# Split-precision mixing and feed-forward products: high and low parts of the activations side by side, five matmuls per step in place of six

## The reference

```python
u = rmsnorm(x, norm_attn); proj = u @ w_in          # attention heads, indexer, state-space heads
h = x + jnp.concatenate([att, y], axis=-1) @ w_out  # mixing product, 2048 x 2048
f = rmsnorm(h, norm_ffn)
h = h + (jax.nn.silu(f @ w_gate) * (f @ w_up)) @ w_down   # hidden width 5632
y = rmsnorm(h, norm_final)
```

## Time and profile before

| | us |
|---|---|
| median of 3 runs | 3274.39 |
| lowest, highest | 3269.07, 3275.76 |
| the profiled execution | 3267.44 |
| its span, first to last instruction | 3265.6 |
| mean granted clock of TensorE | 0.956 |

### The profile page before, as it was taken

How to read it: one execution, slowest core, us unless ns; L and a number is a source line. 1 busy time by engine, 2 the same in 40 slices (tenths; PEclk the granted TensorE clock), 3 DMA queues, 4 the chain that set the end, 5 groups by cost and what they waited for, 6 DMA issues and landing times.

```text
span 3265.6 us, 53293 instructions
## 1 busy us (share of the span) xinstructions
PE 3057.1 (94%) x21743; PEld 2899.3 (89%) x21743; DVE 957.0 (29%) x1714; ACT 763.0 (23%) x1171; POOL 981.5 (30%) x406
## 2 busy tenths in 40 slices
PE   6999997899999996899999999999999999999997
PEld 6887996687777784899999999999999999999997
DVE  2322797434333432212221221221212121121223
ACT  4223222222222222223212121212121112112122
POOL 2322332111111110233333333333333333333331
PEclk8999998998889996899999999999999999999998
DMA  6322223444444443432222222222222222222221
GB/s 186 109 66 72 92 92 91 115 131 139 129 126 117 115 126 114 139 100 93 78 78 86 96 78 78 78 84 98 78 78 78 86 96 78 78 78 89 93 91 59
DMA packets 350273, 317.78 MB, mean 97 GB/s; under 512 B 39821, under 2 KB 319413, under 8 KB 348808
## 3 DMA queue, kind: packets, MB, share of 16 engines
q1 hardware_dynamic: 319368, 293.93, 29.0%
q10 hardware_dynamic: 30720, 21.05, 2.1%
HBM read 284.90 MB, written 31.43 MB: 97 GB/s over the span
## 4 chain that ended last, share of the span: by engine, by line
PE 57%; issue 34%; POOL 7%; ACTq 1%; DVE 1%; ACT 0%; POOLq 0%; DVEq 0%
PE G L705 40%; PE G L1117 17%; POOL WL L634 4%; POOL WL L663 3%; ACTq L1167 0%; ACTq L1168 0%; DVE us L2016 0%; DVE y_out L2035 0%; POOL WL L655 0%; ACT WRAW L1176 0%; PE B L720 0%; ACTq L39 0%; DVE gs L1987 0%; ACT XR L1181 0%; DVE hl L2022 0%
## 5 line engine op out<-in xcount | busy, mean ns | idle before, releaser
L705 PE MATMUL G<-AH,WH 128*128 128x288 f32 (+1 forms) x5024 | 1090.4, 299 | 42.0 <-DVE us L2016 12.2
L705 PE MATMUL G<-AL,WH 128*128 128x288 f32 (+1 forms) x5024 | 1077.9, 296 | 0.0
L705 PE MATMUL G<-AH,WL 128*128 128x288 f32 (+1 forms) x5024 | 1076.5, 296 | 0.0
L705 PEld LDWEIGHTS G<-AH,WH 128*128 128x128 f32 (+1 forms) x5024 | 814.2, 191 | 69.4 <-issue 51.3
L705 PEld LDWEIGHTS G<-AL,WH 128*128 128x128 f32 (+1 forms) x5024 | 814.9, 190 | 0.0
L705 PEld LDWEIGHTS G<-AH,WL 128*128 128x128 f32 (+1 forms) x5024 | 813.4, 190 | 0.0
L655 POOL TENSOR_TENSOR WL<-WRAW,WH 128x1024 fp32r<-128x1024 f32 x208 | 517.4, 2488 | 943.6 <-ACT WH L648 943.6
L648 ACT CAST WH<-WRAW 128x1024 fp32r<-128x1024 f32 x208 | 218.5, 1051 | 1006.6 <-PE G L705 900.1
L653 POOL TENSOR_TENSOR WL<-WRAW,WH 128x1024 fp32r<-128x1024 f32 x88 | 210.8, 2395 | 357.9 <-ACT WH L646 357.9
L1117 PE MATMUL G<-hh,WH 128*128 128x288 f32 x1408 | 303.0, 296 | 4.6 <-DVE hl L2022 4.6
L1117 PE MATMUL G<-hl,WH 128*128 128x288 f32 x1408 | 300.3, 294 | 0.0
(11 more groups left out here) (308 smaller groups left out, 2018.9 us busy)
## 6 DMA issues: line engine op xcount, KB each, us to landing
WRAW<-in_w_gate SPq DMA_DIRECT2D x22, 2048.0 KB
WRAW<-in_w_up SPq DMA_DIRECT2D x22, 2048.0 KB
WRAW<-in_w_down SPq DMA_DIRECT2D x22, 2048.0 KB
WRAW<-in_w_in SPq DMA_DIRECT2D x14, 2048.0 KB, 8.6
raw<-in_w_in SPq DMA_DIRECT2D x48, 512.0 KB, 4.0
kca<-in_cache_k SPq DMA_DIRECT2D x256, 64.0 KB, 2.0
vca<-in_cache_v SPq DMA_DIRECT2D x256, 64.0 KB, 2.0
WRAW<-in_w_out SPq DMA_DIRECT2D x16, 1024.0 KB
```

Source lines behind the costliest of these rows:

```text
L705: last = nc.tensor.matmul(G[gslot][0:width, h, 0:HALF], wt[:, half, k % 8, 0:width], act[:, (k + shift) % KT, h * HALF:(h + 1) * HALF], st ...
```

## The change

AH and AL become one array A3 of 16 blocks x 3 x 384 (WIDE = 384, REST = 96), on the same bytes; hh and hl become H3. A block's three rows hold: 288 high and 96 low values, 288 high and 96 low, 384 low (`highs`, `lows`). Per step, the high weights meet the three rows of 384 (three matmuls into three PSUM banks), the low weights the 288 high values of the first two (two matmuls): `wide_steps`. A result tile F[0] or F[1] has three banks, F[0] being two of the old four single banks with one of G; highs(F) holds the products with high activations, lows(F) those with low ones, and VectorE adds the two. Between dependent VectorE instructions there are new waits (`link`, `Steps` on lo_added). The first mixing tile waits for one more taken tile, the second for the last attention copies; the transposes back use two banks for m < 3. The diff, without its unchanged surroundings and the list of semaphores:

```diff
@@ -18,6 +18,8 @@
 HALF = NT // 2
+WIDE = 2 * NT // 3
+REST = WIDE - HALF
 NH, DH = 8, 128
...
@@ -176,6 +178,9 @@
         top[0] = max(spot["hl"][1], spot["mx"][1])
+        A3 = sb("A3", [P, KT, 3, WIDE], F32R, at=spot["AH"][0])
+        H3 = sb("H3", [P, 4, 3, WIDE], F32R, at=spot["hh"][0])
+        assert spot["A3"][1] == spot["AL"][1] and spot["H3"][1] == spot["hl"][1]
         xt = sb("xt", [P, 2, NT])
...
@@ -187,8 +192,10 @@
-        G = [ctx.enter_context(nc.psum_tensor(f"G{i}", [P, 2, 512], F32)) for i in range(2)]
-        B = [ctx.enter_context(nc.psum_tensor(f"B{i}", [P, 512], F32)) for i in range(4)]
+        PS = ctx.enter_context(nc.psum_tensor("PS", [P, 8, 512], F32))
+        G = [PS[:, 2 * i:2 * i + 2, :] for i in range(2)]
+        B = [PS[:, 4 + i, :] for i in range(4)]
+        F = [PS[:, 3:6, :], PS[:, 0:3, :]]
...
@@ -296,7 +303,7 @@
             for t in range(5):
-                plan(("y", m, t), (5 * m + t) % 4)
+                plan(("y", m, t), 2 + t % 2 if m < 3 else t % 4)
...
@@ -706,6 +713,36 @@
+        def highs(v):
+
+            return v[:, 0:2, 0:HALF]
+
+        def lows(v):
+
+            return v[:, 0:2, HALF:WIDE], v[:, 2, 0:WIDE].rearrange("p (a b) -> p a b", a=2)
+
+        def by_half(v):
+
+            v = v.rearrange("p (a b) -> p a b", a=2)
+            return v[:, :, 0:REST], v[:, :, REST:HALF]
+
+        def wide_steps(out, wh, wl, act, first, last_k):
+
+            for c in range(3):
+                ins = nc.tensor.matmul(out[:, c, 0:WIDE], wh, act[:, c, :], start=first, stop=last_k and c == 2)
+            for c in range(2):
+                ins = nc.tensor.matmul(out[:, c, 0:HALF], wl, act[:, c, 0:HALF], start=False, stop=last_k)
+            return ins
+
+        def wide_half(pe, c, half, slot, shift=0, ready=None):
+
+            pe.wait_ge(s["w_lo"], c + 1)
+            for k in range(8 * half, 8 * half + 8):
+                if ready:
+                    ready(k)
+                last = wide_steps(F[slot], WH[:, half, k % 8, :], WL[:, half, k % 8, :], A3[:, (k + shift) % KT, :, :], k == 0, k == KT - 1)
+            last.then_inc(s["w_used"], 1)
+
         @block.tensor
...
@@ -1095,16 +1132,19 @@
             for n in range(KT):
-                pe.wait_ge(s["tile_taken"], T3 + n - 1)
+                pe.wait_ge(s["tile_taken"], T3 + max(n - 1, 0))
+                if n == 1:
+                    tgiven(pe, "pts", 8)
+                    tgiven(pe, "pvs", 8)
                 for h in range(2):
                     ready = (lambda k: pe.wait_ge(s["mix_lo"], k + 1)) if n == 0 else None
-                    half_unit(pe, C3 + 2 * n + h, h, (T3 + n) % 2, shift=8, ready=ready)
+                    wide_half(pe, C3 + 2 * n + h, h, (T3 + n) % 2, shift=8, ready=ready)
...
                 for h in range(2):
-                    half_unit(pe, c + h, h, slot, ready=ready)
+                    wide_half(pe, c + h, h, slot, ready=ready)
...
@@ -1112,10 +1152,7 @@
                     for k in range(4):
-                        for wt, act in ((WH, hh), (WH, hl), (WL, hh)):
-                            for h in range(2):
-                                last = mm(G[(slot + t) % 2][:, h, 0:HALF], wt[:, half, 2 * k + t, :], act[:, k, h * HALF:(h + 1) * HALF],
-                                          start=(k == 0 and wt is WH and act is hh), stop=(k == 3 and wt is WL))
+                        last = wide_steps(F[(slot + t) % 2], WH[:, half, 2 * k + t, :], WL[:, half, 2 * k + t, :], H3[:, k, :, :], k == 0, k == 3)
                     last.then_inc(s["w_used"] if t else s["d_tile"], 1)
...
@@ -1489,7 +1526,7 @@
                     act.wait_ge(s["w_used"], C3)
-                copy(AH[:, (j + 8) % KT, :], mx[:, j % 6, :]).then_inc(s["m_hi"], 1)
+                copy(highs(A3[:, (j + 8) % KT, :, :]), mx[:, j % 6, :].rearrange("p (a b) -> p a b", a=2)).then_inc(s["m_hi"], 1)
...
@@ -1504,7 +1541,7 @@
                     act.wait_ge(s["tile_taken"], TF)
-                actv(AH[:, k, :], XR[:, k, :], ACT.Copy, scale=gains[:, k:k + 1]).then_inc(s["f_hi"], 1)
+                actv(highs(A3[:, k, :, :]), XR[:, k, :].rearrange("p (a b) -> p a b", a=2), ACT.Copy, scale=gains[:, k:k + 1]).then_inc(s["f_hi"], 1)
             for h in range(2):
...
@@ -1513,7 +1550,7 @@
                     act.wait_ge(s["h_mul"], 4 * g + j + 1)
-                    copy(hh[:, j, :], us[:, j % 2, :]).then_inc(s["hh_done"], 1)
+                    copy(highs(H3[:, j, :, :]), us[:, j % 2, :].rearrange("p (a b) -> p a b", a=2)).then_inc(s["hh_done"], 1)
                 else:
...
@@ -1975,7 +2012,10 @@
                 dve.wait_ge(s["m_hi"], j + 1)
-                tt(AL[:, (j + 8) % KT, :], mx[:, j % 6, :], AH[:, (j + 8) % KT, :].bitcast(F32), ALU.subtract).then_inc(s["mix_lo"], 1)
+                a3 = A3[:, (j + 8) % KT, :, :]
+                for dst, src, hi in zip(lows(a3), by_half(mx[:, j % 6, :]), (a3[:, 0:2, 0:REST], a3[:, 0:2, REST:HALF])):
+                    ins = tt(dst, src, hi.bitcast(F32), ALU.subtract)
+                ins.then_inc(s["mix_lo"], 1)
                 if j + 2 < 8:
...
@@ -1991,7 +2031,11 @@
                 dve.wait_ge(s["w_used"], C3 + 2 * n + 2)
-                tt(two(XR[:, n, :]), G[(T3 + n) % 2][:, :, 0:HALF], two(xt[:, n % 2, :]), ALU.add).then_inc(s["tile_taken"], 1)
+                f3 = F[(T3 + n) % 2]
+                for dst, lo in zip(by_half(xt[:, n % 2, :]), lows(f3)):
+                    ins = tt(dst, dst, lo, ALU.add)
+                link(ins)
+                tt(two(XR[:, n, :]), highs(f3), two(xt[:, n % 2, :]), ALU.add).then_inc(s["tile_taken"], 1)
                 if n:
...
@@ -2001,25 +2045,47 @@
                 dve.wait_ge(s["f_hi"], k + 1)
-                stt(AL[:, k, :], XR[:, k, :], gains[:, k:k + 1], AH[:, k, :].bitcast(F32), ALU.mult, ALU.subtract).then_inc(s["f_lo"], 1)
+                a3 = A3[:, k, :, :]
+                for dst, src, hi in zip(lows(a3), by_half(XR[:, k, :]), (a3[:, 0:2, 0:REST], a3[:, 0:2, REST:HALF])):
+                    ins = stt(dst, src, gains[:, k:k + 1], hi.bitcast(F32), ALU.mult, ALU.subtract)
+                ins.then_inc(s["f_lo"], 1)
             for h in range(2):
...
+            class Steps:
+
+                def start(self, before):
+                    self.before, self.n = before, 0
+
+                def __call__(self, ins):
+                    self.n += 1
+                    ins.then_inc(s["lo_added"], 1)
+                    dve.wait_ge(s["lo_added"], self.before + self.n)
+            lf = Steps()
+
             def take_f(g, j, c, T, slot, up, first=False):
...
                 dve.wait_ge(s["w_used"], c + 2)
-                tt(two(dst), G[slot % 2][:, :, 0:HALF], rstd[:, :, :], ALU.mult).then_inc(s["tile_taken"], 1)
+                f3 = F[slot % 2]
+                for part, lo in zip(by_half(dst), lows(f3)):
+                    ins = cp(part, lo)
+                lf(ins)
+                lf(tt(two(dst), highs(f3), two(dst), ALU.add))
+                tt(two(dst), two(dst), rstd[:, :, :], ALU.mult).then_inc(s["tile_taken"], 1)
                 if up:
...
                     dve.wait_ge(s["hh_done"], 4 * g + j + 1)
-                    tt(hl[:, j, :], dst, hh[:, j, :].bitcast(F32), ALU.subtract).then_inc(s["hl_done"], 1)
+                    h3 = H3[:, j, :, :]
+                    for part, src, hi in zip(lows(h3), by_half(dst), (h3[:, 0:2, 0:REST], h3[:, 0:2, REST:HALF])):
+                        ins = tt(part, src, hi.bitcast(F32), ALU.subtract)
+                    ins.then_inc(s["hl_done"], 1)
...
@@ -2027,17 +2093,23 @@
                     dve.wait_ge(s["d_tile"], tiles + n // 2 + 1)
-                tt(two(XR[:, n, :]), G[slot % 2][:, :, 0:HALF], two(XR[:, n, :]), ALU.add).then_inc(s["tile_taken"], 1)
+                f3 = F[slot % 2]
+                for part, lo in zip(by_half(XR[:, n, :]), lows(f3)):
+                    ins = tt(part, part, lo, ALU.add)
+                lf(ins)
+                tt(two(XR[:, n, :]), highs(f3), two(XR[:, n, :]), ALU.add).then_inc(s["tile_taken"], 1)
             def take_back(m, t):
...
                 taken(tt(y_tok(t)[:, 512 * m:512 * m + 512], bank(name)[0:rows, :], gfin[0:rows, 512 * m:512 * m + 512], ALU.mult), name)
+            lf.start(0)
             for u in range(8):
...
                 c, T, slot = 24 * g + (C3 + 24), 24 * g + (T1 - 24), T1
+                lf.start(32 * g - 16)
                 for f in range(6):
...
@@ -2048,6 +2120,7 @@
                     c = c + 4
+            lf.start(32 * NG - 16)
             for n in range(KT):
```

2 lines of the change are left out of this document (1 added, 1 removed).

## The result

| | us |
|---|---|
| kernel before, median of 4 runs | 3272.87 |
| changed kernel, median of 4 runs (lowest, highest) | 3297.44 (3296.24, 3300.88) |
| ratio, 95% interval | 1.0080 (1.0067 to 1.0094) |
| the profiled execution, its span | 3300.88, 3299.1 |

A forecast was written before the change was run, and what follows sets the result against it. TensorE, busy for 94% of the span, was taken as the bound. -27.6 + 1.2 + 1.2 + 3.0 + 6.5 = -15.7 us from the profiled 3267.4 gave 3251.7; the median's 7.0 us more made 3258.7, range 3180 to 3291.

The forecast's parts named there:

- Matmuls: TensorE's 2368 product steps: five matmuls replace six, one start less per step, 27.6 us saved.
- One excess per step: Each step saves one fixed per-matmul excess over its columns: 13.3, 10 or 12.2 ns by place.
- the proportional rival: Every step: excess grows with columns, so nothing is saved against 11.9 us of costs; 3286 us, chance 0.28.
- the floor: Every step: each matmul takes at least about 130 ns whatever it streams; 101.8 us saved, 3185 us, chance 0.13.
- at its columns: Every step: each matmul runs at its columns plus 2.3 ns; 138.2 us saved, 3148 us, chance 0.07.
- the prediction's own sign: Starts in the trace: 170 ns for 384 columns means fixed, 173 to 177 proportional, 162 floor; 288 at 130.
- Taking a tile: VectorE's take of a result tile becomes three or four instructions, hidden behind TensorE's next tile; cost 0.
- The rival on VectorE: Up tiles: VectorE's multiply meets GpSimd and TensorE waits, 1 us in each of 44 tiles; 3303 us, chance 0.06.
- Split low parts: Two subtractions replace one: 1.2 us at the start of the mixing product, 1.2 at the feed-forward start.
- Exit: Loop exit: TensorE waits 2.2 us more for the last low hidden part, plus 0.8 at the half clock; 3.0 us.
- Transposes: Transposes back on two banks in three of four groups: third, fourth and fifth each wait; 6.5 us.
- Loop turn: The 1.5 us pause at each loop turn belongs to the turn itself and stays; otherwise 30 us on top.

The follow-up runs named there:

- e5: Kernel before with one short matmul of varying width ahead of mixing tiles, first feed-forward tiles and some loop tiles; 3293.3 us.
- e8: Kernel before with its six matmuls of a step in eight orders, tile by tile; 780 to 806.7 ns per step outside the down tiles.
- e7: e3 with the five matmuls of a step in eight orders, tile by tile; 786.7 or 793.3 ns per step in mixing, gate and up tiles.
- e1: Kernel before with each of the sixteen mixing tiles at its own matmul width, 128 to 512 columns; 120.0 ns at 256, 227.0 at 512.
- e3: Changed kernel with gate and up tiles given back after the add, before the multiply; 3283.99 us, 1.0032 of the kernel before.
- e4: Kernel before with only the transposes back put on two PSUM banks for the first three groups; 3279.63 us, 1.0023.
- e12: e3 with order H0 L0 H1 L1 H2 in mixing, gate and up tiles and transposes spread behind down tiles 5 to 15; 3260.53 us, 0.9966.
- e13: Kernel before with the transposes spread on four banks and short matmuls at mixing tile 3 and feed-forward tiles one and eight; 3264.23 us, 0.9980.
- e2: Kernel before, single mixing tiles changed in one thing each (weights, moving operand, bank, type); two-byte 109.3 ns at 256 columns, others 131.6 to 135.1 at 288.
- e9: Kernel before with a 32-column matmul ahead of mixing tile 2, feed-forward tile 1 and inside each turn's first tile; 3275.29 us, 1.0004.
- e11: e3 with order H0 L0 H1 L1 H2 in mixing, gate and up tiles and eight orders in the loop's down tiles; 3269.77 us, one run.

## Why the prediction was wrong

**1. Matmuls (-27.6 us): the step that failed.** "One excess per step" took the distances 133.3 and 130.0 as a price per start. The runs showed a price that the sequence sets as a whole: 60 or 80 ns a step over its columns for the same six matmuls by how the stream was entered (e5), 73 in the down tiles, 60 to 87 by their order (e8), 73 or 67 for five (e7). In a stream of one width the excess stays at 12 to 16 ns from 256 to 512 columns (e1), so the proportional rival (117 and 234 ns forecast by it at 256 and 512, 120.0 and 227.0 measured) is refuted too, and so are the floor and "at its columns". By the prediction's own sign (173 to 177 ns for 384 columns) the changed kernel's 176.7 would have spoken for the proportional rival; only the ladder tells them apart. The change's order fell on the poorer of its two values, and it gave up the 780 of 960 steps, the best value that any run showed for a steady step. The clue was used only half: the unequal distance for the same instruction on the same operands was read as "a handover", and it was a sign that the distance is no property of a matmul. Measured +3.4 us, an error of 31.0.

**2. Taking a tile (cost 0): failed.** The pieces were right (353, 546 and 757 ns in their groups against 350, 556 and 760; the multiply 2.48 us), and the 4.1 us after which the multiply ends is what the trace shows. But the cover was checked for the next weight conversion only. Who else waits for the tile, the down tile of 3.1 us behind it, was worked out for the down take and not for the last gate tile of f = 0, whose banks the second down tile takes. e3 measures it: 13.4 us. The rival on VectorE named the mechanism, at the up tiles with 2.8 us to spare; its place was wrong. The Trainium skill (SBUF — State Buffer, "SBUF: two separate sides") says that a VectorE instruction with two SBUF inputs and a GpSimd one that reads SBUF shut each other out; the trace agrees: 2.47 us for the multiply beside GpSimd's 2.38, and 0.76 for the add that reads PSUM.

**3. Split low parts (1.2 + 1.2): near in size, not in mechanism.** The start of mixing was to cost 0.16 us per block. It cost 2.2 us at once, as the second subtraction met GpSimd's, and gave 1.4 back in the first tile beyond what its steps gain: 0.8. That the sum comes near 1.2 is luck. The wait at the feed-forward start went from 5.3 to 6.0, +0.7.

**4. Exit (3.0): right but for the clock.** 6.61 us idle in place of 4.55, +2.1 with 2.2 forecast. Of the 0.8 for a longer stretch at the half clock the trace has 0.2: the first tile behind the exit takes 5.4 us in place of 5.2.

**5. Transposes (6.5): right alone, too low in the changed kernel.** 6.3 in e4's trace, 8.2 in its medians, which have 4.3 to 10.8 as interval; two waits in a group of five, where three were forecast. In the changed kernel itself the last down products and what follows took 8.9 us more than before. 1.1 of that is the tile behind the first burst, for the granted clock was 0.5 there from 3239.6 to 3243.0 us; it fell while TensorE stood for the second time in the burst, and so it did in five of the six traces of this form with bursts, but not in e4. That the cost was the burst of five, and not the two banks, e12 and e13 show.

**6. Loop turn.** The pause didn't grow, as forecast; it fell from 14.2 to 9.3 us over nine turns. It belongs to the form and not to the execution: 12.9 to 14.2 us in the eight traces with six matmuls, 8.1 to 10.5 in the seven with five. No run looked into that, and the cause is open.

Sum of the forecast and its errors: -15.7 + 31.0 (point 1) + 13.4 (2) - 0.4 - 0.5 (3) - 0.9 (4) + 2.8 (5: 8.9 and the 0.4 that its steps gained, less 6.5) - 4.9 (6) = +24.8, as measured. (The prediction's chance of "faster" is 0.57; its own parts add up to 0.59.) Of the change's 24.6 us, e3 took back 13.4, the order 9.6, and the spread transposes 13.9, which puts the five-matmul form 12.3 us under the kernel before.

## What to carry to other kernels

In these streams a start-to-start distance is a property of the whole repeating sequence and of where it stands, not of the matmul: where a trace shows the same instruction at two paces, look at the pattern of single distances, and try orders of the sequence, before counting what fewer starts would save. When an instruction is split in two, see what the second one meets: here GpSimd, for 2.2 us. When a result buffer is given back later, follow it to the next tile that needs that buffer for every kind of tile that can stand between, the shortest above all. A burst of transposes that shares few banks can be spread into the products around it at the cost of a reordered queue: 10.7 us here on two banks by the traces (13.9 by the medians, other differences included), 2.7 on four.

## What the runs showed of the hardware that was not expected

- In a stream, float32r matmuls go 12 to 16 ns over one column per cycle from 256 to 512 columns, two-byte ones 2.6 at 256 (e1, e2); from 224 columns down to 128, with 128 x 128 float32r weights, the distance stays at 111.5 ns.
- Steady distances of a step come in grains: 780, 786.7, 790, 793.3, 800 and 806.7 ns, all multiples of 3.33. Outside the down tiles the same six matmuls have two stable patterns, 131 131 132 140 and 132 128. A short matmul can turn one into the other, after the stop at the turn of the loop the stream always came back at 800 (nine turns in each of the traces of the kernel before, e1, e2, e4, e9 and e13), and sixteen down tiles swap the two (both ways in e9 and e13). The order that is the slower one in mixing, gate and up tiles is the faster one in down tiles (e7, e11). What in TensorE keeps such a state, no run here shows.
